# Two neural blocks on one core: SBUF buffers at multiples of 256 bytes, one reciprocal for four groups, and the order of work around it

## The reference, cut to what matters

```python
def reference(x, ...):                    # x (1, 512, 1024), float32
    h = layer_norm(x)                     # first block
    u = h @ w_in                          # split: u_glu, z, xbc, dt, gate_a, gate_b
    y_a = silu(layer_norm(dwconv31(a * sigmoid(g)))) @ w_conv_out     # a, g = halves of u_glu
    xbc = silu(dwconv4(xbc))              # xs, B, C
    y   = ssd_chunked(xs, dt, B, C) + xs * d_skip      # scan over 4 chunks of 128, 4 groups
    yg  = (y * silu(z)).reshape(..., 4, 512)
    yg  = yg * rsqrt(mean(yg**2, axis=-1) + 1e-5)      # one scale per token and group
    y_b = (yg * norm_w) @ w_ssm_out
    mix = (sigmoid(gate_a) * y_a + sigmoid(gate_b) * y_b) @ w_o
    h = layer_norm(2**0.25 * h + mix)
    h = layer_norm(2**0.25 * h + (silu(gate) * val) @ w_ffn_down)     # gate, val = dwconv3(h @ w_ffn_up)
    h = concat(meta_tokens, h)            # second block: 16 + 512 positions
    for l in range(2):                    # windowed attention and a gated conv, out, then an MLP
        h = h + rmsnorm(concat(rmsnorm(attn), rmsnorm(conv)) @ w_out[l])
        h = h + rmsnorm(relu(rmsnorm(h) @ w_up[l])**2 @ w_down[l])
    return h[:, 16:]
```

## The kernel before

| buffer | before | after |
|---|---|---|
| whi, wlo, raw (both slots), ahi, alo | 160 | 0 |
| yn_hi, yn_lo, chi, clo, mixhi, mixlo, fhi, flo, f2hi, f2lo | 96 | 0 |
| const1 (ident, ones) | 128 | 0 |
| y_tok and diag (line 842) | 224 | 128 |
| vout, res1 | 32 | 192 |

## Time and profile before

### The profile page before, as it was taken

How to read it: one execution, slowest core, us unless ns; L and a number is a source line. 1 busy time by engine, 2 the same in 40 slices (tenths; PEclk the granted TensorE clock), 3 DMA queues, 4 the chain that set the end, 5 groups by cost and what they waited for, 6 DMA issues and landing times.

```text
span 2443.6 us, 35569 instructions
## 1 busy us (share of the span) xinstructions
PE 2311.2 (95%) x13200; PEld 1998.6 (82%) x13200; DVE 1467.8 (60%) x1690; ACT 1014.0 (41%) x1391; POOL 128.4 (5%) x77
## 2 busy tenths in 40 slices
PE   7998999978999999999999999999999999999996
PEld 6776777756777788888899989999998987888885
DVE  6757888799866556554665466225346656632544
ACT  5456666552242555532535443223222454422321
POOL 0000000123000000000200020000010002000000
PEclk9999999988999999999999999999999999999998
DMA  3222223212222122233211112222222111222221
GB/s 149 86 96 85 92 86 95 89 52 76 96 87 87 56 99 98 91 138 136 79 67 53 52 64 92 87 86 86 96 77 90 53 35 69 89 101 87 102 87 51
DMA packets 34499, 207.55 MB, mean 85 GB/s; under 512 B 4802, under 2 KB 4802, under 8 KB 10980
## 3 DMA queue, kind: packets, MB, share of 16 engines
q1 hardware_dynamic: 28128, 194.66, 22.3%
q10 hardware_dynamic: 6276, 11.57, 1.7%
HBM read 204.05 MB, written 2.17 MB: 84 GB/s over the span
## 4 chain that ended last, share of the span: by engine, by line
PE 71%; DVE 15%; DVEq 7%; ACT 4%; issue 3%; ACTq 1%; DMA 0%; POOL 0%; POOLq 0%
PE PS L478 22%; PE PS L482 22%; PE PS L480 22%; DVEq L1587 2%; DVE vout L1594 2%; DVE wlo L1400 2%; ACT whi L909 1%; PE PS L807 1%; DVEq L1488 1%; DVE hres L1489 1%; PE PS L833 1%; DVE zres L1487 1%; DVE rstd L1479 1%; DVEq L1524 1%; DVE xbc L1520 1%
## 5 line engine op out<-in xcount | busy, mean ns | idle before, releaser
L478 PE MATMUL PS<-ahi,whi 128*128 128x512 f32 (+1 forms) x2472 | 753.7, 345 | 27.7 <-DVE alo L1473 12.1
L482 PE MATMUL PS<-ahi,wlo 128*128 128x512 f32 (+1 forms) x2472 | 739.8, 339 | 0.0
L480 PE MATMUL PS<-alo,whi 128*128 128x512 f32 (+1 forms) x2472 | 739.7, 339 | 0.0
L1400 DVE TENSOR_TENSOR wlo<-raw,whi 128x2048 fp32r<-128x2048 f32 x176 | 404.2, 2297 | 504.1 <-ACT whi L909 504.1
L909 ACT ACTIVATE whi<-raw 128x2048 fp32r<-128x2048 f32 x179 | 342.8, 1915 | 729.8 <-PE PS L482 724.7
L478 PEld LDWEIGHTS PS<-ahi,whi 128*128 128x128 f32 x2472 | 426.2, 189 | 98.2 <-issue 30.3
L482 PEld LDWEIGHTS PS<-ahi,wlo 128*128 128x128 f32 x2472 | 425.4, 189 | 51.0
L480 PEld LDWEIGHTS PS<-alo,whi 128*128 128x128 f32 x2472 | 425.3, 188 | 50.6 <-issue 1.9
L480 PE MATMUL PS<-f2lo,whi 128*128 128x264 f32 (+1 forms) x768 | 205.8, 322 | 0.0
L482 PE MATMUL PS<-f2hi,wlo 128*128 128x264 f32 (+1 forms) x768 | 205.7, 322 | 0.0
L478 PE MATMUL PS<-f2hi,whi 128*128 128x264 f32 (+1 forms) x768 | 205.5, 322 | 0.0
(11 more groups left out here) (253 smaller groups left out, 2759.8 us busy)
## 6 DMA issues: line engine op xcount, KB each, us to landing
raw<-weights SPq DMA_DIRECT2D x181, 1024.0 KB, 4.8
acs_b<-acs_rows ACTq DMA_DIRECT2D x34, 256.0 KB, 3.3
const<-const ACTq DMA_DIRECT2D x2, 1232.0 KB, 5.4
x_in<-x_t SPq DMA_DIRECT2D x4, 512.0 KB, 4.9
out_t<-hres SPq DMA_DIRECT2D x8, 256.0 KB, 2.0
cols<-columns SPq DMA_DIRECT2D x1, 385.0 KB, 6.7
const<-const SPq DMA_DIRECT2D x1, 256.0 KB, 6.3
acs_rows<-dtt ACTq DMA_DIRECT2D x1, 64.0 KB
```

Of the source, the lines that this page charges most:

```text
L478: nc.tensor.matmul(o, wh, h, start=first, stop=False)
L480: nc.tensor.matmul(o, wh, h, start=False, stop=False)
L482: mm = nc.tensor.matmul(out[j], wl, hi[j], start=False, stop=last)
L1400: v.tensor_tensor(wlo[s][:, :], raw[s][:, :], whi[s][:, :].bitcast(F32), ALU.subtract).then_inc(lo_ready, 1)
```

## The change

It has three parts. (1) Every buffer that `fixed` hands out, `R` and `H0` start at multiples of 256 bytes. (2) The norm over groups: ACT squares into four buffers (`ysq4`) and does all 16 before the first `gate`; DVE sums all 16 before making any `wlo`; the four group sums go through 32 columns of ones each into one bank, 32 partitions a group; one root, one reciprocal `rst` for the four groups; PE spreads each group's row back over 128 partitions, again with ones, into banks 4 to 7, from which DVE scales. The sums stand inside unit 1 of `gate_b` (before: unit 2), the new small matmuls inside unit 2. (3) In `ssm_out` DVE does one round of taps, then `wlo`, one round, the product with `gb`, then the remaining rounds; before, all rounds came first.

```diff
-        top = [1152]
+        top = [1280]
         def fixed(name, n, dt=F32):
-            top[0] += 4 * n
+            top[0] += 4 * n + (-4 * n) % 256
...
-        H0 = (R_END - R - 4 * KD * L) // 32 * 32
+        H0 = (R_END - R - 4 * KD * L) // 256 * 256
...
                 for g in range(GROUPS):
-                    mm = nc.tensor.matmul(bank(4 + g), ones, sumsq[:, g * T:(g + 1) * T], start=True, stop=True)
+                    mm = nc.tensor.matmul(PS[32 * g:32 * g + 32, 4 * 512:5 * 512], ones[:, 0:32],
+                                          sumsq[:, g * T:(g + 1) * T], start=True, stop=True)
                 mm.then_inc(ss_ps, 1)
+            def group_scales():
+                pe.wait_ge(ss_rec, 1)
+                for g in range(GROUPS):
+                    r = slice(32 * g, 32 * g + 1)
+                    nc.tensor.matmul(bank(4 + g), ones[r, :], rst[r, :], start=True, stop=True).then_inc(ss_bc, 1)
...
             def conv_mean():
-                pe.wait_ge(ss_std, GROUPS)
+                pe.wait_ge(y_normed, XT)
...
-            linear(PLAN["gate_b"], ahi, alo, T, amid={2: group_sums})
+            linear(PLAN["gate_b"], ahi, alo, T, amid={1: group_sums, 2: group_scales})
...
             act.wait_ge(yg_ok, XT)
-            y_squares(0, XT // 2)
+            for k in range(XT):
+                y_square(k)
             gate(stage, 0, gb)
-            y_squares(XT // 2, XT)
+            act.wait_ge(ss_ps, 1)
+            nc.scalar.activation(rst[:, :], bank(4), ACT.Sqrt, bias=col("eps5", 0), scale=1.0 / (GP * P)
+                                 ).then_inc(ss_std, 1)
             gate(stage, 1, gb)
...
+            low_at(stage_b.u0 + 2)
             long_taps(odd, 0, TAPS_GATE)
+            dve.wait_ge(ss_std, 1)
+            v.reciprocal(rst[:, :], rst[:, :]).then_inc(ss_rec, 1)
+            low_at(stage_b.u0 + 3)
...
                 if k % GP == 0:
-                    dve.wait_ge(ss_std, k // GP + 1)
-                    v.reciprocal(rst4[:, g], rst4[:, g])
-                    drain()
-                v.scalar_tensor_tensor(xbc[:, c], xbc[:, c], col("ssm_norm", k), rst4[:, k // GP * T:(k // GP + 1) * T],
+                    dve.wait_ge(ss_bc, k // GP + 1)
+                v.scalar_tensor_tensor(xbc[:, c], xbc[:, c], col("ssm_norm", k), bank(4 + k // GP),
                                        ALU.mult, ALU.mult).then_inc(y_normed, 1)
...
-                    long_taps(odd, (n + 1) // 2 * s, n if s else (n + 1) // 2, n * i + TAPS_GATE)
+                    w0, w1 = (n + 1) // 2 * s, n if s else (n + 1) // 2
+                    long_taps(odd, w0, w0 + 1, n * i + TAPS_GATE)
                     low_next(stage_s, i, s)
+                    long_taps(odd, w0 + 1, w0 + 2, n * i + TAPS_GATE)
                     hold(dve, ring_ok, 2 * i + (s + 1), "dve")
                     t = cut(gb, 2 * T * i + s * T, T)
                     v.tensor_tensor(t, t, ring[s][:, :], ALU.mult).then_inc(ring_used, 1)
+                    long_taps(odd, w0 + 2, w1, n * i + TAPS_GATE)
```

More of the change, by code:

```diff
@@ L146, in build @@
         alo = fixed("alo", KD * L, F32R)
-        mu, std, rstd = fixed("mu", L), fixed("std", L), fixed("rstd", L)
-        R = top[0]
+        mu, std, rstd = (nc.alloc_sbuf_tensor_at(name, [P, L], F32, offset=top[0] + 4 * L * j)
+                         for j, name in enumerate(("mu", "std", "rstd")))
+        R = top[0] + 12 * L + (-12 * L) % 256
         R_END = 228200 // 32 * 32
@@ L182, in build @@
         t0 = ssd0 + 16 * TB
-        rst4 = sumsq = at("sumsq", t0, 4 * T)
+        sumsq = at("sumsq", t0, 4 * T)
+        rst = at("rst", t0, T)
         ring = [at(f"ring{s}", t0 + s * TB, T) for s in range(2)]
         ysq = [at(f"ysq{s}", t0 + (4 + s) * TB, T) for s in range(2)]
+        ysq4 = [at(f"ysq4{s}", ssd0 + s * TB, T) for s in range(4)]
         prod = ysq + [at("prod2", v0, T)]
@@ L328, in build @@
         zs_ok, yg_ok, ysq_ok, ysq_sum = sem("zs_ok"), sem("yg_ok"), sem("ysq_ok"), sem("ysq_sum")
-        ss_ps, ss_std = sem("ss_ps"), sem("ss_std")
+        ss_ps, ss_std, ss_rec, ss_bc = sem("ss_ps"), sem("ss_std"), sem("ss_rec"), sem("ss_bc")
         y_normed, yhi_ok, ylo_ok = sem("y_normed"), sem("yhi_ok"), sem("ylo_ok")
@@ L1097, in _, with y_square @@
                 act.wait_ge(acs_in[s], 16 * (HEADS // 2 + 1))
[L1100 to L1105, removed]
+            def y_square(k):
+                if k >= 4:
+                    act.wait_ge(ysq_sum, k - 3)
+                nc.scalar.activation(ysq4[k % 4][:, :], xbc[:, k * T:(k + 1) * T], ACT.Square).then_inc(ysq_ok, 1)
             def gate(stage, u, dst):
@@ L1670, in _ @@
             stage_b = PLAN["gate_b"]
[L1671 to L1678, removed]
-                            drain()
-                            v.tensor_tensor(acc, acc, ysq[j % 2][:, :], ALU.add).then_inc(ysq_sum, 1)
-                low_at(stage_b.u0 + half + 2)
+            for k in range(XT):
+                dve.wait_ge(ysq_ok, k + 1)
+                acc = sumsq[:, k // GP * T:(k // GP + 1) * T]
+                if k % GP == 0:
+                    v.tensor_copy(acc, ysq4[0][:, :]).then_inc(ysq_sum, 1)
+                else:
+                    drain()
+                    v.tensor_tensor(acc, acc, ysq4[k % 4][:, :], ALU.add).then_inc(ysq_sum, 1)
+            low_at(stage_b.u0 + 2)
             long_taps(odd, 0, TAPS_GATE)
+            dve.wait_ge(ss_std, 1)
+            v.reciprocal(rst[:, :], rst[:, :]).then_inc(ss_rec, 1)
+            low_at(stage_b.u0 + 3)
             def y_low(k):
@@ L1695, in _ @@
                 if k % GP == 0:
-                    g = slice(k // GP * T, (k // GP + 1) * T)
-                    dve.wait_ge(ss_std, k // GP + 1)
-                    v.reciprocal(rst4[:, g], rst4[:, g])
-                    drain()
-                v.scalar_tensor_tensor(xbc[:, c], xbc[:, c], col("ssm_norm", k), rst4[:, k // GP * T:(k // GP + 1) * T],
+                    dve.wait_ge(ss_bc, k // GP + 1)
+                v.scalar_tensor_tensor(xbc[:, c], xbc[:, c], col("ssm_norm", k), bank(4 + k // GP),
                                        ALU.mult, ALU.mult).then_inc(y_normed, 1)
```

## The result

The changed kernel takes **2429.56 us** (median of 4 runs, 2427.72 to 2432.16), the kernel before on the same chip 2448.15: ratio **0.9931**, 95% interval 0.9919 to 0.9942, about 17 us faster. The forecast was 2431.5. The profiled execution has a span of 2427.0 us, 16.6 less than before. Where they arose (starts and ends of the stages in both traces): 5.2 us by the start of `conv_out`, then 2.05 in `conv_out` (0.9 by the addresses, 1.1 by the early `wlo`, see e1, e2 and e5), 1.3 in `w_o`, 3.0 in `ffn_down` and twice 2.55 in layer 1's `down`. What is left nearly cancels: 1.6 us won in `ffn_up`, where the clock did not fall this time, 1.2 lost in layer 1 before its first `down`, 0.3 in layer 0.

What follows compares the result with a forecast made beforehand. PE's price per matmul was taken as the bound, DVE from 466 to 655 us. Addresses -12.0, norm and early `wlo` -3.8: -15.8 from 2445.4 gives 2429.6, plus 1.9 to the median 2431.5 us; 8-in-10 range 2416 to 2446.

Steps and rivals of the forecast that it cites:

- What bounds: Whole kernel: PE's price per matmul sets the time, except from 466 to 655 us, where DVE is the chain.
- Part 1, distance modulo 256: 512-column matmuls: 13.3 ns lost where moving operand and weights start at distance 0, 20 ns elsewhere; 1680 x 6.67 ns = 11.2 us.
- `yn` at nothing: The 384 matmuls on `yn`, 2.6 us, lie where DVE is the bound, so their new addresses gain nothing.
- The -0.8 for layer 0's `f2hi`: Layer 0's 1536 matmuls of 264 columns on `f2hi` get 0.7 ns cheaper; 0.8 us taken, 0 to 1.1.
- Part 2, -0.8 at the last `yn_lo`: Norm: the last `yn_lo` ends 0.8 us earlier, at 534.3, as DVE newly waits for PE's units 2 and 3.
- the bound of -5: Norm: lower bound if sums and spreading cost a quarter by using separate parts of the array.
- Part 3, the mean moves by DVE alone: Conv mean in `gate_a`: follows DVE's last sum, so it moves only by DVE's 0.8 us despite PE being early.
- Part 3, "behind it -3": Behind the mean: DVE's 2.83 us wait for `whi` goes, and ACT's root and PE's unit 3 follow by 3 us.
- (a): Rival, all matmuls: absolute alignment to 64 counts too, most of the loss goes; 150 us at most, 2295; chance 0.08.
- (d): Rival: the moving operand's own address counts, 160 good, others bad; +13.5 us, 2461; chance 0.08.
- (b): Rival: new addresses do nothing, the price belongs to the stage; only -3.8 us, 2443.5; chance 0.08.
- (c): Rival, norm: PE idles 5.8 us in unit 1, then runs at 1.2 GHz (+7); 2439 with the new addresses; chance 0.08.

Runs made afterwards that it cites:

- e1: The kernel before with only the new 256-byte addresses; median 9.7 us below that of the kernel before beside it (2446.06).
- e2: The changed kernel with the old addresses, so the norm and early `wlo` alone; median 6.6 us below that of the kernel before (2446.06).
- e5: The changed kernel with the `wlo` of `ssm_out` back behind its rounds of taps; median 4.6 us above the changed kernel's.
- after: The changed kernel itself, with all three parts, against the kernel before; 2429.56 us, ratio 0.9931.
- e3: The changed kernel with every buffer 32 bytes higher, distances kept; as fast as the changed kernel.
- e4: The changed kernel with weights, and what lies before them, starting at 128 modulo 256, other operands left; 15 us slower than the changed kernel.
- e7: The changed kernel with layer 1's `ahi` and `alo` packed without the 64 bytes between tiles; median 3.5 us below the changed kernel's.
- e8: Whole computation left out: PE alone runs matmul series at chosen start addresses, some alternating places by turns; a single execution of 427.1 us.
- e6: The changed kernel with the norm's sums and spreading products on the whole array, none side by side; last `yn_lo` ends at 535.3 us, against 530.7.
- e12: e7 with 12 dummy products, `spin(12)`, on PE before the mean of the conv; median 2423.4 us.

## Why the prediction was right, and where its terms were off

- **What bounds: right.** Both readings held, PE's price outside and DVE's chain from 466 to 655 us (e5: a wait of 12 us of PE costs 1.1 there).
- **Part 1, distance modulo 256: right in mechanism, nearly in size.** Forecast -11.2 for the 512-column stages; e1's stages show 10.4, `chi` and `fhi` 0.4 less each than their counts. `after` has 11.4 in the same stages, of which 1.1 in `conv_out` is part 3's, as e2 has it at the old addresses. e3, e4, e7 and e8 show the mechanism; only "the distance" of one matmul's own operands doesn't tell all (e8, by turns). The Trainium skill's page "SBUF — State Buffer", section "Who interferes with whom", gives PE two independent read ports, by which the distance should not matter. The same runs don't agree (226.7 against 233.3 ns). `yn` at nothing: it lies ahead of the mean, which DVE sets.
- **The -0.8 for layer 0's `f2hi`: wrong in sign.** It stayed at 122.4 and `ahi` rose to it; layer 0 gives back 0.3 to 1 us. The distances at the halves' starts, from which I took it, aren't what counts.
- **Part 2, -0.8 at the last `yn_lo`: mis-sized, -4.4 measured.** I kept 5.4 and 3.4 us for eight half products "as they have as many moving columns", with the packing as the bound of -5. 1.93 and 1.14 are true: with 32 columns or one row of the array each, four run beside one another. e6, with my durations, ends where I forecast, wait by wait. The Trainium skill, page "TensorEngine Tiling (Array Packing)", section "Theoretical Speedup", gives up to 4 times for a dimension of 32 or less. The rows show 3.59/1.14 = 3.1 for the spreading; the 5.40/1.93 = 2.8 of the sums has 1.93 at 1.2 GHz throughout and 5.40 only in part. From one four to the next at 1.2 GHz it is 0.85 us, as much as from one product to the next in e6: four times. That end should have had more weight in the forecast.
- **Part 3, the mean moves by DVE alone: nearly right.** DVE's last sum came 5.1 us earlier and the mean 5.7. The forecast read the mean in the earlier trace rows as one that waits for that sum; it had no wait and PE came last.
- **Part 3, "behind it -3": mis-sized, -1.1 measured** (19.8 to 18.7 us from DVE's last sum to `rstd`). The wait of 2.83 us went, as forecast. The step that failed is that PE's and ACT's work follows by 3 of it. PE being early meant a wait of 2.6 us before the mean, the clock fell to 1.2 GHz behind it, and DVE's next `wlo` stood 2.74 us for 0.93. e12, which fills that wait, has 2.8 of the 3 (17.1).
- **The sum was met partly by luck.** In the traces part 1 with layer 0 gave 10.0 us for 12.0, parts 2 and 3 gave 6.2 (5.2 by the start of `conv_out`, 1.1 in it) for 3.8, and the falls of the clock 0.4: 16.6 for 15.8, from errors of opposite sign.
- **Rivals.** (a), (d) refuted by e3, (b) by the rows above. (c) had its clock right (behind the wait of 4.41 us PE ran at 1.2 GHz, 0.43 us a matmul until 482.95) and its price wrong: the sums took 1.93 us.

## What to carry to other kernels

Count how many matmuls a stretch without waits begins: where the same shape has two prices at the same clock, look at the starts of moving operand and weights modulo 256 and bring them to the same, whatever that is, for every tile and from one matmul to the next (a stride that is no multiple of 256 loses it for most). Small products that each use a strip of rows or columns run four at a time, so price them by the array that they fill, not by their moving columns. When an engine is made early for a wait that another engine ends, fill the wait with dummies of its measured length, counted from a row and not by name.

## What was not expected of the hardware

- Distance 64 costs a third of what others do (229.2 against 233.3, with 226.7 at 0), and 8 or 16 bytes off are already off (233.5 and 231.9, or 230.9 and 233.4 with the weights that much higher).
- Distance 0 in every matmul is not enough: where both operands change their place together from one matmul to the next, the step is 233.4.
- Four strips at once: eight half products of 512 float32 columns in 1.93 us (32 columns of weights, all at 1.2 GHz) and in 1.14 (one row, at 2.4 GHz), against 5.40 (partly at 1.2 GHz) and 3.59 with the whole array.
- Behind the same wait the granted clock falls in one execution and not in another, where the code around it is the same: 1.4 to 4.7 us each time, at three places of this kernel.
